# Alternating two heads that use different halves of the array, in the second block's attention products

## The reference, cut to what matters

```python
for layer in range(DEPTH):                       # DEPTH = 2
    h = rms_norm_2(x, norm_gain[layer])
    proj = h @ w_in[layer]                       # q, k, v (4 mixers x 8 heads x 64), gate, 8 forget logits
    o_a = dilated_attention(rope(norm(q[0])), rope(norm(k[0])), v[0])
    o_b = stick_breaking_attention(q[1], k[1], v[1])
    o_c = moba_attention(rope(norm(q[2])), rope(norm(k[2])), v[2])
    o_d = forgetting_attention(norm(q[3]), norm(k[3]), v[3], log_f)
    y = concat(o_a, o_b, o_c, o_d) * silu(gate)
    x = x + y @ w_out[layer]

def forgetting_attention(q, k, v, log_f):        # the running sums are cum
    cum = cumsum(log_f)
    s = q @ k.T * SCALE + cum[:, None] - cum[None, :]
    return softmax(where(key <= query, s, NEG)) @ v
```

## Time and profile before

| | us |
|---|---|
| median of 3 runs (lowest to highest) | 3090.27 (3089.97 to 3090.63) |
| the profiled execution | 3088.68 |
| its span, first to last instruction | 3086.9 |
| TensorE, matmuls busy | 3072.2 |
| VectorE busy | 1856.9 |
| ScalarE busy | 1602.9 |

### The profile page before, as it was taken

One profiled execution on the slowest core, in us unless ns is written; L12 is line 12 of the kernel. 1 busy time (PEld: TensorE's weight loads), 2 busy tenths in 40 slices (PEclk: granted clock), 3 DMA queues, 4 the chain that ended last, 5 costly groups with the idle time before them and its releaser, 6 DMA issues.

```text
span 3086.9 us, 60516 instructions
## 1 busy us (share of the span) xinstructions
PE 3072.2 (100%) x25980; PEld 3042.8 (99%) x25980; DVE 1856.9 (60%) x2028; ACT 1602.9 (52%) x2085; POOL 0.2 (0%) x4
## 2 busy tenths in 40 slices
PE   9999999999999999999999999999999999999999
PEld 9999999999999999999999999999999999999999
DVE  7655555444555478765554555557667666766664
ACT  7654544333443366754443344447556655656663
POOL 0000000000000000000000000000000000000000
PEclk9999999999999999999999999999999999999999
DMA  7335555645556455565566565656656556656654
GB/s 241 115 127 177 177 177 177 198 156 174 178 178 200 154 176 173 175 200 191 190 211 199 170 196 191 218 177 172 183 166 178 172 170 192 178 173 176 173 163 149
DMA packets 530944, 551.10 MB, mean 179 GB/s; under 512 B 15472, under 2 KB 524528, under 8 KB 529648
## 3 DMA queue, kind: packets, MB, share of 16 engines
q1 hardware_dynamic: 530800, 549.00, 56.9%
HBM read 541.56 MB, written 2.10 MB: 176 GB/s over the span
## 4 chain that ended last, share of the span: by engine, by line
PE 95%; ACT 2%; DVE 2%; issue 1%; DMA 0%; SPq 0%; DVEq 0%; ACTq 0%
PE ps L676 87%; PE ps L746 2%; PE ps L1106 1%; PE ps L1018 1%; PE ps L814 1%; PE ps L1009 1%; PE ps L1026 0%; PE ps L985 0%; PE ps L924 0%; ACT w_hi L1134 0%; ACT w_hi L1141 0%; PE ps L845 0%; PE ps L819 0%; DVE w_lo L1663 0%; DMA raw<-mla_w_in_dram 0%
## 5 line engine op out<-in xcount | busy, mean ns | idle before, releaser
L676 PE MATMUL ps<-x_all,w_hi 128*128 128x256 f32 (+1 forms) x11672 | 2062.1, 281 | 7.2 <-DVE xb L2051 3.8
L676 PEld LDWEIGHTS ps<-x_all,w_hi 128*128 128x128 f32 x11672 | 1782.9, 188 | 15.6 <-issue 9.7
L676 PE MATMUL ps<-x_all,w_lo 128*128 128x256 f32 (+1 forms) x5836 | 1635.0, 280 | 0.0
L676 PEld LDWEIGHTS ps<-x_all,w_lo 128*128 128x128 f32 x5836 | 1098.5, 188 | 0.0
L1663 DVE TENSOR_TENSOR w_lo<-raw,w_hi 128x1024 fp32r<-128x1024 f32 (+3 forms) x496 | 650.9, 1314 | 548.2 <-ACT w_hi L1141 548.1
L1141 ACT ACTIVATE w_hi<-raw 128x1024 fp32r<-128x1024 f32 (+3 forms) x496 | 560.2, 1131 | 643.1 <-PE ps L676 626.6
L1657 DVE TENSOR_TENSOR w_lo<-raw,w_hi 128x1024 fp32r<-128x1024 f32 (+2 forms) x496 | 595.3, 1202 | 485.3 <-ACT w_hi L1134 481.6
L1134 ACT ACTIVATE w_hi<-raw 128x1024 fp32r<-128x1024 f32 (+2 forms) x496 | 513.3, 1037 | 369.6 <-PE ps L676 366.3
L676 PE MATMUL ps<-hid_hi,w_lo 128*128 128x272 f32 (+1 forms) x1408 | 397.4, 282 | 0.0
L676 PE MATMUL ps<-hid_hi,w_hi 128*128 128x272 f32 (+1 forms) x1408 | 397.0, 282 | 0.0
L676 PE MATMUL ps<-hid_lo,w_hi 128*128 128x272 f32 (+1 forms) x1408 | 396.6, 282 | 0.0
(11 more groups left out here) (294 smaller groups left out, 2125.9 us busy)
## 6 DMA issues: line engine op xcount, KB each, us to landing
raw<-ffn_w_gu_dram SPq DMA_DIRECT2D x176, 1024.0 KB, 5.0
raw<-w_in_dram SPq DMA_DIRECT2D x128, 1024.0 KB, 5.4
raw<-ffn_w_down_dram SPq DMA_DIRECT2D x64, 1408.0 KB, 6.5
raw<-w_out_dram SPq DMA_DIRECT2D x32, 1024.0 KB, 5.4
raw<-lru_w_in_dram SPq DMA_DIRECT2D x24, 1024.0 KB, 5.5
raw<-mla_w_o_dram SPq DMA_DIRECT2D x16, 1024.0 KB, 5.4
raw<-lru_w_o_dram SPq DMA_DIRECT2D x16, 1024.0 KB, 5.3
raw<-lru_y_gates_dram SPq DMA_DIRECT2D x8, 1280.0 KB, 5.6
```

Source lines behind the costliest of these rows:

```text
L676: mm = pe.matmul(out, l, r, start=first and k == 0 and i == 0, stop=last and k == kn - 1 and i == 2)
```

## The change

The order of the products changes, on TensorE alone, in two functions. In `scores2` the four heads are taken in pairs, (0, 1) and (2, 3), and within a pair each product is issued for both heads before the next one: first queries of both, then (forgetting units) `cum_hi` of both, `cum_lo` of both, then the second queries of both, and their running sums likewise. In `values2` the first key tile is issued for both heads of a pair, then the second. The products themselves, their operands and their places in the accumulator stay, and so does the order of the products of any one head. The diff:

```diff
--- before.py
+++ after.py
@@ -968,24 +968,36 @@
                         pe.wait_ge(rows_made, 1 + layer)
                     if u > 0:
                         pe.wait_ge(y_made, u + UNITS * layer)
-                    for hd in range(4):
+                    def of_head(hd):
                         rows = slice(64 * (hd % 2), 64 * (hd % 2) + 64)
-                        q, k = qk[rows, hd // 2, :], qk[rows, 2 + hd // 2, :]
+                        select = sel_r[rows, 4 * (u % 2) + hd:4 * (u % 2) + hd + 1].broadcast_to([HD, P])
+                        return rows, qk[rows, hd // 2, :], qk[rows, 2 + hd // 2, :], select
+
+                    def first_queries(hd):
+                        rows, q, k, select = of_head(hd)
                         if m == 1:
-                            pe.matmul(ps[:, 4 + hd, 256:384], k[:, P:256], q[:, P:256], start=True, stop=True)
-                            mm = pe.matmul(ps[:, 4 + hd, 0:256], k[:, 0:P], q, start=True, stop=True)
-                            continue
-                        low, high = ps[:, 4 + hd, 0:128], ps[:, 4 + hd, 128:384]
-                        forget = m == 3
-                        select = sel_r[rows, 4 * (u % 2) + hd:4 * (u % 2) + hd + 1].broadcast_to([HD, P])
-                        mm = pe.matmul(low, q[:, 0:P], k[:, 0:P], start=True, stop=not forget)
-                        if forget:
-                            pe.matmul(low, select, cum_hi[rows, 0:P], start=False, stop=False)
-                            pe.matmul(low, select, cum_lo[rows, 0:P], start=False, stop=True)
-                        mm = pe.matmul(high, q[:, P:256], k, start=True, stop=not forget)
-                        if forget:
-                            pe.matmul(high, select, cum_hi[rows, :], start=False, stop=False)
-                            mm = pe.matmul(high, select, cum_lo[rows, :], start=False, stop=True)
+                            return pe.matmul(ps[:, 4 + hd, 256:384], k[:, P:256], q[:, P:256], start=True, stop=True)
+                        return pe.matmul(ps[:, 4 + hd, 0:128], q[:, 0:P], k[:, 0:P], start=True, stop=m != 3)
+
+                    def second_queries(hd):
+                        rows, q, k, select = of_head(hd)
+                        if m == 1:
+                            return pe.matmul(ps[:, 4 + hd, 0:256], k[:, 0:P], q, start=True, stop=True)
+                        return pe.matmul(ps[:, 4 + hd, 128:384], q[:, P:256], k, start=True, stop=m != 3)
+
+                    def running_sums(hd, at, rows_of, last):
+                        rows, q, k, select = of_head(hd)
+                        n = at.stop - at.start
+                        return pe.matmul(ps[:, 4 + hd, at], select, rows_of[rows, 0:n], start=False, stop=last)
+
+                    for two in ((0, 1), (2, 3)):
+                        for of, at in ((first_queries, slice(0, 128)), (second_queries, slice(128, 384))):
+                            for hd in two:
+                                mm = of(hd)
+                            if m == 3:
+                                for rows_of in (cum_hi, cum_lo):
+                                    for hd in two:
+                                        mm = running_sums(hd, at, rows_of, rows_of is cum_lo)
                     mm.then_inc(s_made, 1)
 
                 def turn_probs2(u):
@@ -1011,12 +1023,12 @@
 
                 def values2(u):
                     pe.wait_ge(pt_ready, 2 * (u + 1 + UNITS * layer))
-                    for hd in range(4):
-                        c = hd // 2
-                        out = ps[64 * (hd % 2):64 * (hd % 2) + 64, 4, 256 * c:256 * c + 256]
-                        vh = slice(64 * hd, 64 * hd + 64)
-                        pe.matmul(out, v2[:, 0, vh], p2[:, hd, 0:256], start=True, stop=False)
-                        mm = pe.matmul(out[:, P:256], v2[:, 1, vh], p2[:, hd, 256:384], start=False, stop=True)
+                    for c in range(2):
+                        for kt in range(2):
+                            for hd in (2 * c, 2 * c + 1):
+                                out = ps[64 * (hd % 2):64 * (hd % 2) + 64, 4, 256 * c + P * kt:256 * c + 256]
+                                mm = pe.matmul(out, v2[:, kt, 64 * hd:64 * hd + 64], p2[:, hd, 256 * kt:256 + P * kt],
+                                               start=kt == 0, stop=kt == 1)
                     mm.then_inc(o_made, 1)
 
                 def both_parts(table, first_bank):
```

## The result

The changed kernel took 3095.61 us (median of 20 runs, 3094.46 to 3096.54), the kernel before, beside it, 3090.33 us (20 runs, 3089.76 to 3091.02): ratio 1.0017 with an interval of 1.0011 to 1.0023, 5.28 us slower. The forecast was 3086.5 us with a range up to 3089.4; the time moved the other way and out of the range.

A forecast was written before the change was run, and what follows sets the result against it. TensorE was taken to bound the kernel; removing half B's lag gives 1.20 us (short scores) + 1.96 (running sums) + 0.64 (values) = 3.80 us, so 3086.5 us from 3090.27, range 3085.2 to 3089.4.

The forecast's parts named there:

- what the places would become: Durations of short scores, scores with running sums, and values: about 1.51, 2.44 and 1.46 us, from 1.61, 2.93 and 1.51.
- the engine already ran the halves beside each other: Array halves A (heads 0, 2) and B (heads 1, 3) already overlap out of program order; second load 0.01 us behind.
- B's lag: Half B (heads 1, 3) finishes behind half A by 0.11, 0.50 or 0.05 us per place; all but 0.01 recoverable.
- running sums of both halves meet without harm: Running sums of both array halves now coincide in scores; taken as free, at worst +2.9 us net if they took turns.
- 1: Rival: only the long lag, in scores with running sums, goes; 3088.3 us; chance 13%.
- 2: Rival: no lag goes, since queue speed in handing out instructions sets half B's lag; 3090.3 us; chance 4%.
- A's last starts: Last matmul starts of half A (heads 0, 2), forecast unmoved at 1.20, 2.22 and 1.25 us after a place began.
- 3: Rival: each of 192 more changes of half costs time; at 30 ns, 3092.2 us; 5% with running sums taking turns.
- Rival 4: Matmuls start only in program order, lengthening short scores and values; +6.8 us, 3097.1 us; chance 2%.
- 5: Rival: two tiles at once halve the 55 us of scores and values; 3063 us; within 2% for more gain.
- time taken out of TensorE's stream in the second block comes off the end almost one for one: Step from TensorE's matmuls covering 3072.2 of 3086.9 us: the places' 3.80 us should come off the kernel.
- A wait at L676: Where 0.1 to 0.5 us per place would return if the cover for the next projection's weights were gone; not expected.

The follow-up runs named there:

- e5: The changed kernel with the last of the four products of the heads' sums of squares issued as two of 256 columns: 3090.26 us, ratio 1.0004.
- e6: The changed kernel, but in the values heads 2 and 3 go back to the old order, only heads 0 and 1 alternating: 3091.4 us, ratio 1.0006.
- e8: The kernel before with only the twelve short scores (those without running sums) alternating: 3089.07 us, ratio 0.9999.
- e12: e8 with the very first unit's scores in the old order too: 3088.98 us, ratio 0.9995.
- e4: The kernel before with only the scores and their running sums alternating, values in the old order: 3088.48 us, ratio 0.9995.
- e9: e4 with the first unit in the old order and head 3's last running sum issued as two products of 128 columns: 3088.41 us, ratio 0.9994.
- e3: The kernel before with only the values alternating, scores in the old order: 3099.26 us, ratio 1.003.
- e11: e4 with the first unit in the old order and the second pair of forgetting heads taken as 3, 2: 3088.68 us, ratio 0.9995.
- e14: The changed kernel with head 3's last value product issued as two of 64 columns, so half B ends later: 3096.28 us, ratio 1.0021.
- e10: The kernel before, old order everywhere, with the last product of the heads' sums of squares issued as two of 256 columns: ratio 1.0002, +0.53 us.
- e13: The changed kernel with six 256-column products issued as twelve of 128, 54 matmuls into the 144 stretch, units 1 to 7: 3109.0 us, ratio 1.0059.

## Why the prediction was wrong

**Right: what the places would become.** Forecast 1.51, 2.44 and 1.46 us, measured 1.51, 2.43 and 1.45; forecast gain 3.80 us, measured 4.05. That the engine already ran the halves beside each other, that only B's lag was to be had, and that running sums of both halves meet without harm, all held.

**Right against the rivals.** The lags went in all three kinds of places (1 and 2 fall). A's last starts stayed at 1.20, 2.21 and 1.25 us behind the start of a place, so changes of half cost nothing that shows (3 falls) and the starts do not follow the program's order, which would have put the first one at 1.54 (4 falls). Nothing was halved (5). Rival 4 came near the measured time, 3097.1 against 3095.61, by luck: its mechanism is not in the trace.

**Wrong: "time taken out of TensorE's stream in the second block comes off the end almost one for one".** That step took the projections between the places to be a constant. They are not: a matmul of them takes 113.3 or 117.8 ns, which of the two depends on what ran ahead, and 9.3 us hung on the order that was changed. A wait at L676, which I had named as what would have taken the gain if the places were shorter and the kernel was not, took none of it: the waits of TensorE come to 11.7 us, against 11.3.

**It could have been read.** The chain of before has 16.96 us for one stretch of 144 matmuls beside 16.33 for the others. I read the places instruction by instruction and no piece of the chain between them. Two lengths for the same work, with no wait in either, would have told that the pace could change, and the stretches of 144, 192 and 48 that are at the short pace in before would have given a price on the slower side: some 14 x 0.63 + 14 x 0.83 + 10 x 0.2 = 22 us if all of them turned long.

**Shown, and open.** Shown: the pace is taken where a stretch begins or is interrupted, kept to its end, and moved by edits of the products just ahead of it (e5, e6, e8 with e12, e4 with e9); what ran ahead of those products counts too (e3, and after beside e4). Open: what about an ending makes it long. Neither the later half (e11) nor the gap between the halves' ends (e14) is it, a split that helps in one place does nothing or harm in another (e5, e10, e13), and I have no rule that foretells an entry from its instructions. The trace shows only that the rhythm differs by some ns ahead of the stretch already: in unit 5 of layer 0 the four sums of squares start 231, 236 and 231 ns apart before, and 236, 229 and 231 after.

## What to carry to other kernels

When a small reordering is to be worth a few us in a kernel that one engine bounds, price its neighbours too: list the pieces of the chain that do identical work and see whether they come in more than one length. If they do, judge the edit by their sum, since 0.63 us in a stretch of 16.33 outweighs the 0.05 to 0.50 us that a place gains. And try an edit in its parts, because the gain of one (the scores, -1.42 us) can hide behind the loss of another (the values, +9.36).

## What the runs showed of the hardware that I had not expected

A stream of load and matmul pairs with 256 columns has two paces, 113.3 and 117.8 ns, 4% apart, at a granted clock of 1.00; it stays at one for 48 to 192 matmuls unless it is interrupted (e13). The Trainium skill (TensorE: Matmul & The Clock Gate, Back-to-back issue gap) gives one gap for each number of columns; by its formula for an isolated matmul an estimate for 256 columns is 256 / 2.4 + 2.5 = 109 ns. The short pace here is 4% above that, the long one 8%, and the trace does not agree with there being only one.

Twelve matmuls of 128 columns, each with a load of its own, took 1.29 us (e13), 108 ns each, hardly less than one of 256 columns: in that stream halving a product nearly doubles it. And changes of the half from one product to the next cost nothing that the trace shows: with 7 of them instead of 3, half A's last start still comes 1.20 us after the place began.
